# A joint first stage, a state-space scan whose inputs are fetched in the stage ahead of it, and a reordered preparation stage in a kernel of two networks

## What is computed

```python
# first block, layer 0: projections of x; attention with a bias by relative distance
proj = jnp.einsum('bsd,df->bsf', h, w_in)          # h is x, 1024 x 1024
bias = rel_bias[_t5_bucket(off * dilation)]
# second block: the conditioning vectors
sc, scc = jax.nn.silu(c), jax.nn.silu(c_ctx)[None]

def ssd_stream(z, xbc, dt_raw, ...):               # state-space branch
    xbc = silu(dwconv_centred(xbc, conv_w) + conv_b)
    xs, bm, cm = split(xbc)
    # forward and backward chunked scans of xs * dt, with the decays exp(cumsum(dt * a))
    y = y_f + flip(y_b) + d_skip[:, None] * xs
    return rms_norm(y * silu(z), norm_g)

def gdn_stream(qkv, gate, ...):                    # gated delta rule branch
    q, k = l2_norm(q) * 64 ** -0.5, l2_norm(k)
    ...                                            # both directions, one state per head
    return rms_norm(o_f + flip(o_b), norm_g) * silu(gate)
# the gdn branch walks the 16 x 64 grid of tokens by columns; its result is put back in raster order
lat = concatenate([pool_branch(...), s_lat, to_raster(g_lat)]) @ w_out
```

## Time and profile before

| | |
|---|---|
| median of 3 runs | 4337.53 us (4337.32 to 4341.66) |
| the profiled execution | 4332.35 us, of which 4330.8 us are the span from the first to the last instruction |
| mean granted TensorE clock over the span | 0.918 of full speed |
| PE busy, VectorE busy, ScalarE busy, GpSimd busy | 3677.2, 1645.7, 1081.7, 1009.2 us |
| start of the program to the first product of the projection | 0 to 46.0 us |
| `gdn_prepare` starts | 2930.4 us |
| `gdn_scan` loads start, `ssd_scan` starts, `pool_branch` starts | 3351.8, 3492.4, 3651.2 us |

### The profile page before, as it was taken

One profiled execution on the slowest core, in us unless ns is written; L12 is line 12 of the kernel. 1 busy time (PEld: TensorE's weight loads), 2 busy tenths in 40 slices (PEclk: granted clock), 3 DMA queues, 4 the chain that ended last, 5 costly groups with the idle time before them and its releaser, 6 DMA issues. The chain is left out here.

```text
span 4330.8 us, 47294 instructions
## 1 busy us (share of the span) xinstructions
PE 3677.2 (85%) x16689; PEld 2393.0 (55%) x16689; DVE 1645.7 (38%) x3931; ACT 1081.7 (25%) x2192; POOL 1009.2 (23%) x844
## 2 busy tenths in 40 slices
PE   7989998889798999999989598997867835757996
PEld 3635676667345566656568346574456834333442
DVE  1025552432442335345443251324478546141101
ACT  0023343332332233323321350221113111111111
POOL 0000000332341333333332353002222533111110
PEclk9989999899899999999999797998988857878998
DMA  3164532221531111111111532122325421445996
GB/s 97 63 182 140 167 101 80 95 69 55 213 128 49 43 57 42 58 38 39 43 59 44 232 130 78 44 70 89 117 79 179 158 82 35 173 172 200 319 324 218
DMA packets 413680, 494.03 MB, mean 114 GB/s; under 512 B 71298, under 2 KB 319386, under 8 KB 413459
## 3 DMA queue, kind: packets, MB, share of 16 engines
q1 hardware_dynamic: 384947, 457.61, 32.0%
q0 software_dynamic: 4608, 16.78, 1.5%
q10 hardware_dynamic: 23904, 16.78, 1.2%
HBM read 362.32 MB, written 128.77 MB: 113 GB/s over the span
## 5 line engine op out<-in xcount | busy, mean ns | idle before, releaser
L628 PE MATMUL hgrn_ps_w<-xT,hgrn_ring 128*128 128x512 f32 x1152 | 508.7, 597 | 0.0
L600 POOL TENSOR_TENSOR hgrn_queries<-hgrn_qd,hgrn_pair_decay 128x640 f32<-128x640 f32 x192 | 284.5, 1499 | 416.9 <-PE hgrn_ps_a L679 196.9
L628 PEld LDWEIGHTS hgrn_ps_w<-xT,hgrn_ring 128*128 128x128 f32 x1152 | 217.4, 193 | 252.4 <-issue 252.4
L624 PE MATMUL hgrn_ps_w<-hgrn_ring,xT 128*128 128x256 f32 x1536 | 337.9, 379 | 0.0
L624 PEld LDWEIGHTS hgrn_ps_w<-hgrn_ring,xT 128*128 128x128 f32 x1536 | 289.2, 190 | 38.2 <-issue 0.5
L780 DVE COPY_PREDICATED hgrn_scores<-hgrn_mask,hgrn_ps_s 128x128 f32<-128x128 uint32 x192 | 48.7, 297 | 469.9 <-issue 468.5
L352 PE MATMUL gla_bg_ps<-gla_bg_w,xT 128*128 128x256 f32 x768 | 195.8, 401 | 5.3 <-DMA gla_bg_w<-in_w_in_ab_dram 5.3
L352 PEld LDWEIGHTS gla_bg_ps<-gla_bg_w,xT 128*128 128x128 f32 x768 | 151.3, 202 | 38.7 <-issue 10.6
L1145 PE MATMUL end_ps_z<-end_w,end_yT 128*128 128x512 f32 x384 | 168.6, 599 | 1.6 <-ACT end_yT L1094 1.6
L878 ACT ACTIVATE hgrn_k_tok<-hgrn_ps_a 128x256 f32<-128x256 f32 x84 | 32.2, 383 | 547.9 <-PE hgrn_ps_a L654 547.9
L2292 PE MATMUL end_ps_z<-end_w,end_yT 128*128 128x512 f32 x384 | 167.4, 596 | 0.8 <-ACT end_yT L2220 0.8
(11 more groups left out here) (596 smaller groups left out, 6785.5 us busy)
## 6 DMA issues: line engine op xcount, KB each, us to landing
expw_wg<-in_exp_w_gate_dram SPq DMA_DIRECT2D x16, 2048.0 KB, 10.5
expw_wu<-in_exp_w_up_dram SPq DMA_DIRECT2D x16, 2048.0 KB, 16.2
expw_wd<-in_exp_w_down_dram SPq DMA_DIRECT2D x16, 2048.0 KB, 21.8
att_w_ada<-in_ada_w_dram SPq DMA_DIRECT2D x24, 1024.0 KB, 6.1
hgrn_ring<-in_w_in_c_dram SPq DMA_DIRECT2D x36, 512.0 KB, 4.0
end_gt<-gate_l SPq DMA_DIRECT2D x16, 768.0 KB, 7.4
hgrn_ring<-in_w_in_c_dram SPq DMA_DIRECT2D x12, 1024.0 KB, 5.4
hgrn_o<-hgrn_o_stage SPq DMA_DIRECT2D x192, 64.0 KB, 2.8
```

What stands on the lines that cost most here:

```text
L600: pool.tensor_tensor(queries[:, d, s, :].rearrange("p (b a c) -> p b a c", b=POINTS, a=PC), q, f, ALU.mult).then_inc(queries_done, 1)
L624: last = pe.matmul(bank[:, q * 2 * P:(q + 1) * 2 * P], xT[:, k, t * P:(t + 1) * P], wt[:, k, :], start=(k == 0), stop=(k == KB - 1))
L628: last = pe.matmul(bank[:, :], wt[:, k, 0:P], xT[:, k, part * BANK:(part + 1) * BANK], start=(k == 0), stop=(k == KB - 1))
```

## The change

Six edits, in the order of the program.

1. `transpose_in`, `bias_vectors` and `condition` become one stage, `prologue`. All eight tiles of x have a buffer of their own, so no load waits. The first two weight blocks of the projection, the conditioning vectors and the clearing of `vpad` are issued behind them on the same queue; the two tables come through ACT's queue. ACT copies every second bank. PE makes the three bias products after the fifth tile. `project` gets the two weight buffers already filled.
2. In `gdn_prepare` the first background weight block is asked for ahead of k and q, the other two behind; ACT's moves of the lead stand ahead of the roots.
3. `gdn_scan` stores each finished tile with one DMA of 128 partitions, in column order; `mix_and_route` reads `y_gdn` with two DMAs of 64 partitions per tile, in raster order.
4. Five of the six inputs of `ssd_scan` are loaded inside `gdn_scan`, one per step from the third on, behind that step's own loads. They lie in the memory of `hT`, which is free by then, and in one new tensor.
5. In `ssd_scan` the products `xdt` and `xw` are made unit by unit: four ahead, the others among the takes of the context units (DVE) and inside the loop over latent units (POOL), where the eight skip products stand too.
6. The gate's Silu stands behind the sixteen Exp on ACT and waits only for the gate.

```diff
+def prologue(nc, tag, src, dst, rel_bias, buckets, vectors, vpad, c, c_ctx, sT, weights, wbuf):
...
+        raw = sb("raw", [P, T, D])
...
+        @block.sync
+        def _(sp):
+            for t in range(T):
+                sp.dma_start(raw[:, t, :], src[t * P:(t + 1) * P, :]).then_inc(raw_loaded[t], 16)
+            for b in range(2):
+                sp.dma_start(wbuf[b][:, :, :], weights.rearrange("(k p) n -> p k n", p=P)[:, :, b * W:(b + 1) * W]).then_inc(w_loaded, 16)
...
+                sp.dma_start(cond[:, 0, :], c[0].rearrange("(k p) -> p k", p=P)).then_inc(cond_loaded, 16)
+                sp.dma_start(cond[:, 1, :], c_ctx.rearrange("(k p) -> p k", p=P)).then_inc(cond_loaded, 16)
+            sp.wait_ge(zeroed, 2)
+            for first in (0, P, VPAD + SEQ, VPAD + SEQ + P):
+                sp.dma_start(vpad[first:first + P, :], zero[:, :]).then_inc(stored, 16)
+            sp.wait_ge(w_loaded, 32)
...
+        @block.scalar
+        def _(act):
+            act.dma_start(rb[0:REL_BUCKETS, :], rel_bias).then_inc(bias_loaded, 16)
+            act.dma_start(bk[:, :], buckets).then_inc(bias_loaded, 16)
             for t in range(T):
...
+                act.activation(dst[:, 4:8, t * P:(t + 1) * P], ps[n % 5][:, :].rearrange("p (j c) -> p j c", j=4), ACT.Copy).then_inc(act_copied, 1)
+            act.wait_ge(cond_loaded, 32)
+            act.activation(sT[:, :, :], cond[:, :, :].rearrange("p r k -> p k r"), ACT.Silu)
+            act.wait_ge(scaled, 3)
+            act.dma_start(vectors, vec[:, :]).then_inc(stored, 16)
+            act.wait_ge(stored, 80)
...
+                if t == MIDDLE:
+                    pe.wait_ge(bias_loaded, 32)
+                    pe.wait_ge(zeroed, 2)
+                    for n in range(3):
+                        pe.matmul(ps_v[n][0:AH, 0:VEC], rb[:, :], bk[:, n * VEC:(n + 1) * VEC], start=True, stop=True).then_inc(made, 1)
...
             def load(job, i, u, f, before, column):
-
+                if u < held:
+                    return
...
@@ ssd_scan: POOL @@
-            pool.wait_ge(loaded, 96)
-            for d in range(2):
-                pool.wait_ge(xdt_done, T2 * (d + 1))
-                for t in range(T2):
-                    pool.tensor_tensor(by_head(xw[:, d, t, :]), by_head(xdt[:, d, t, :]),
-                                       spread(to_end[:, t, d * SH:(d + 1) * SH], SH, SE), ALU.mult).then_inc(xw_done, 1)
-            for t in range(TILES):
-                pool.tensor_tensor(by_head(Y[:, t, :]), by_head(xs[:, t, :]), spread(skip[:, :], SH, SE), ALU.mult).then_inc(y_set, 1)
...
+            for u in range(AHEAD):
+                weigh(u)
             for n in range(LAT_UNITS):
...
                 last.then_inc(sm_done, 1)
+                if n < LAT_UNITS - 2:
+                    weigh(n + AHEAD)
+                if n < TILES:
+                    skip_path(n)
                 if n:
                     pool.drain()
                     add(n - 1)
@@ ssd_scan: VectorE @@
+            weigh(0, AHEAD)
+            dve.wait_ge(consts, 1)
             args(0)
+            weigh(AHEAD, AHEAD + 4)
             for u in range(2 * CTX_STEPS):
                 take(u)
+                weigh(AHEAD + 4 + 3 * u, AHEAD + 7 + 3 * u)
@@ ssd_scan: ScalarE @@
-            act.wait_ge(loaded, 96)
-            act.activation(gate[:, :, :], gate[:, :, :], ACT.Silu).then_inc(gate_done, 1)
             for n in range(LAT_UNITS):
                 act.wait_ge(arg_done, n + 1)
                 act.activation(sm[:, n % 2, :, :], sm[:, n % 2, :, :], ACT.Exp).then_inc(exp_done, 1)
+            act.wait_ge(loaded, 16)
+            act.activation(gate[:, :, :], gate[:, :, :], ACT.Silu).then_inc(gate_done, 1)
@@ gdn_prepare @@
+            bg.load(sp, 0)
             for n, dst in ((1, k_n), (0, q_n)):
                 sp.dma_start(dst[:, :, :], tok[:, n * GW:(n + 1) * GW].rearrange("(t p) c -> p t c", p=P)).then_inc(loaded, 16)
-            bg.begin(sp)
+            for u in range(1, bg.ring):
+                bg.load(sp, u)
...
+            for g in range(LEAD):
+                bg.move(act, g)
             act.wait_ge(squared, 2 * T2)
             act.wait_ge(consts, 1)
             act.activation(std[:, :, :], norms[:, :, :], ACT.Sqrt, bias=eps[:, 0:1]).then_inc(std_done, 1)
-            for g in range(LEAD):
-                bg.move(act, g)
@@ gdn_scan @@
+                if 0 <= s - FIRST < len(next_loads):
+                    dst, src = next_loads[s - FIRST]
+                    sp.dma_start(dst, src).then_inc(fetched, 16)
...
-                    for w in range(P // GRID_H):
-                        sp.dma_start(y_out.rearrange("(r t w) c -> w r t c", t=TILES, w=P // GRID_H)[w, :, t, :],
-                                     O[w * GRID_H:(w + 1) * GRID_H, t, :]).then_inc(stored, 16)
-            sp.wait_ge(stored, 16 * TILES * (P // GRID_H))
+                    sp.dma_start(y_out[t * P:(t + 1) * P, :], O[:, t, :]).then_inc(stored, 16)
+            sp.wait_ge(stored, 16 * TILES)
+            sp.wait_ge(fetched, 16 * len(next_loads))
@@ mix_and_route @@
-                for src, dst in ((y_ssd, y[:, t % 2, 0, :]), (y_gdn, y[:, t % 2, 1, :]), (x, xt[:, t % 2, :])):
+                for src, dst in ((y_ssd, y[:, t % 2, 0, :]), (x, xt[:, t % 2, :])):
                     sp.dma_start(dst, src[rows, :]).then_inc(loaded[t % 2], 16)
+                for r in range(P // GRID_W):
+                    sp.dma_start(y[r * GRID_W:(r + 1) * GRID_W, t % 2, 1, :],
+                                 y_gdn.rearrange("(w r) c -> r w c", r=GRID_H)[t * (P // GRID_W) + r]).then_inc(loaded[t % 2], 16)
```

More of the change, by code:

```diff
@@ L173, in multiply @@
             def multiply(job, i, u, f, before, column):
-                wait(pe, w_loaded[u % 2], 16 * i + 16 * (u // 2 + 1))
+                wait(pe, w_loaded[u % 2], 16 * i + 16 * (u // 2 + 1) - 8 * held)
                 w = wbuf[u % 2]
@@ L2878, in by_head, with ssd_inputs, ssd_scan @@
     return t.rearrange("p (h e) -> p h e", e=width)
-def ssd_scan(nc, tag, tok, chan, z, d_skip, norm_g, dt, cum, from_start, to_end, whole, logs, y_out):
+def ssd_inputs(hT, bc_T, tok, chan, d_skip, norm_g):
     BC = 2 * N_STATE
+    flat = hT[:, :, :].rearrange("p k t -> p (k t)")
+    ends = (T2 * SW, T2 * (SW + BC), T2 * (SW + BC) + SH, T2 * (SW + BC) + SH + SW)
+    xs = flat[:, 0:ends[0]].rearrange("p (t c) -> p t c", c=SW)
+    b_tok = flat[:, ends[0]:ends[1]].rearrange("p (t c) -> p t c", c=BC)
+    skip, norm = flat[:, ends[1]:ends[2]], flat[:, ends[2]:ends[3]]
+    rows = lambda a: a.rearrange("(t p) c -> p t c", p=P)
+    loads = ((xs, rows(tok[:, 0:SW])), (b_tok, rows(tok[:, SW:SW + BC])), (bc_T[:, :, :], chan.rearrange("(k p) t -> p k t", p=P)),
+             (skip, row_to_all(d_skip, SH)), (norm, row_to_all(norm_g, SW)))
+    return (xs, b_tok, bc_T, skip, norm), loads
+def ssd_scan(nc, tag, inputs, z, dt, cum, from_start, to_end, whole, logs, y_out):
     HG = SH // 2 * SE
+    AHEAD = 2 * CTX_STEPS
     with ExitStack() as ctx:
@@ L2889, in ssd_scan @@
         pbank = lambda n: ctx.enter_context(nc.psum_tensor(f"{tag}_{n}", [P, BANK], F32))
[L2890 to L2891 removed]
+        xs, b_tok, bc_T, skip, norm = inputs
         gate = sb("gate", [P, TILES, SW])
[L2893 removed]
         mask = sb("mask", [P, 2, P])
@@ L3014, in _, with weigh @@
         def _(dve):
-            dve.wait_ge(loaded, 96)
-            dve.wait_ge(consts, 1)
-            for d in range(2):
-                for t in range(T2):
+            def weigh(first, last):
+                for u in range(first, last):
+                    t, d = place(u)
                     dve.tensor_tensor(by_head(xdt[:, d, t, :]), by_head(xs[:, t, :]), spread(dt[:, t, d * SH:(d + 1) * SH], SH, SE),
```

152 lines of the change are left out of this document (59 added, 93 removed).

## The result

| | before | after |
|---|---|---|
| median | 4337.42 us | 4256.06 us |
| fastest to slowest | 4328.48 to 4341.66 | 4250.86 to 4259.29 |
| profiled execution, its span | 4332.35, 4330.8 | 4256.28, 4254.6 |

What follows compares the result with a forecast made beforehand. Stages kept apart by barriers take turns waiting, with PE and DMA not full early on. Gains 21.0 + 7.6 + 9.9 - 0.3 + 31.3 = 69.5 us take 4332.35 to 4262.9, median 4268; range 4254 to 4284 (0.75), or to 4290.

Steps and rivals of the forecast that it cites:

- Start of the program: Joint first stage: bytes moved set its end, first product at 25.0 instead of 46.0 us; gain 21.0, bounds 17 and 22.5.
- Preparation: Delta rule's preparation: earlier weights and ACT moves bring the first turns 9.6 us earlier; gain 7.6 us, bounds 5 and 9.6.
- the price of PE's pause: Preparation: PE's pause of 8 us ahead of the loop costs about 2 us once more.
- Stores: Delta rule's end: 64 store issues become 8, next stage starts at 3482.5; gain 9.9 us, bounds 9 and 10.2.
- Fetching ahead: Delta rule's scan: loading 6.1 MB of state-space inputs there hides in free DMA time; cost 0, bounds 0 and 4 us.
- Held-up steps: Rival: added loads make one or two delta rule steps wait, total 4272 to 4276 us; chance 0.05.
- State-space scan: State-space stage: a shorter head less a longer loop; gain 31.3 us, bounds 23.5 and 38.
- The head: State-space scan's head: second unit's arguments at S+22.9 instead of S+60.2, 37.3 us less; bounds 34 and 41.
- The loop: State-space loop: `ssd_kept` waits for GpSimd's products, 6 us longer, between 3 and 10.5.
- Its signs: State-space loop: 5.2 to 5.8 us per unit for eight units, 5.1 to 5.4 behind, `ssd_kept` mean above 1 us.
- The rival in which VectorE waits for all of GpSimd's row: State-space loop: VectorE gets in only after GpSimd's whole piece, 41 us more instead of 6, total 4303; chance 0.10.
- the one in which all engines take turns: State-space loop: the three engines' work adds to 13.2 us per unit, 130 us more, total 4392; chance 0.02.

Runs made afterwards that it cites:

- e8: Changed kernel with the four padding stores moved into the projection and the bias table stored ahead of the conditioning vectors: first product at 22.53 us, median 4254.29 us.
- e7: Changed kernel with the preparation's 20 squares made by ACT and VectorE's drains there removed: stage 164.6 us, median 4244.02 us, ratio to before 0.9783.
- e12: Kernel before with ACT's moves ahead of the norms, weights still asked for behind k and q: preparation 175.6 us, ratio 0.9985.
- e11: Kernel before with only the delta rule's stores in raster order and the mixing stage's reads to match: stage 130.8 us, ratio 0.9978.
- e4: Kernel before with the state-space inputs fetched in the delta rule's scan, all products still made ahead of the loop: state-space stage 138.2 us, ratio 0.9949.
- e1: Kernel before with the joint first stage alone: first product at 25.35 us, ratio 0.9958.
- e3: Kernel before with xdt, xw and skip products made by unit, inputs still loaded at the state-space stage's start: stage 139.4 us, ratio 0.9952.
- e5: Changed kernel with one added GpSimd product per unit in 14 units of the state-space loop: loop 85.6 us, ratio to before 0.9833.
- e6: Changed kernel with three added GpSimd products per unit in 14 units of the state-space loop: loop 102.5 us, ratio to before 0.9876.
- e10: Changed kernel with six added GpSimd products per unit in the first eight state-space units, a row of eight: stage 154.3 us, ratio to before 0.9899.

## Why the prediction was right, and where its terms were off

The direction, the order of the terms and the range held; 76.1 us came for 69.5, and 4256 for 4268. Of these 12 us, 6.6 are gain beyond the forecast and 5.2 the allowance of the median over the profiled execution, which the kernel before had and the changed kernel has not. The stated range reaches down to 4254, so that it held with 2 us to spare, and in part by luck: the state-space scan gained more than its upper bound and the preparation less than its lower one. The lower sum of the bounds, 54 us, also leaves out the 4 us of the fetching; with them it is 50.

**Start of the program**, forecast 21.0, measured 20.7 and, alone, 20.6 (19.9 on average against all old starts). The sum of bytes was right: 340 to 426 GB/s, a hole of 1 us for the vectors. The padding, put at 3.0 us, adds 2.7 (e8); without it the vectors' slow way would set the end.

**Preparation**, forecast 7.6, measured 4.8 and 5.1, at or below the forecast's lower bound. The turns come 9.4 us earlier, as worked out (9.6), and VectorE's chain is what is late next. The step that failed is the price of PE's pause: 2 us were taken from the comparison of 16 records of a fill, and it is 4.4 (e7). The fill of the kernel before, from which the price came, stood behind a pause too, but PE was busy without a break behind it, the granted clock was at 0.95 again in the stretch from 2973 to 2974, and the decays that followed at 2978 took their 1.50 us. Here turns, a wait and decays follow, the clock stays at 0.50 beyond 2960, and turns, decays and the next fill take 0.90, 2.93 and 3.93 in place of 0.49, 1.50 and 2.74. And the forecast took both edits as gains. e12 shows that asking for the weights first costs 3.8 us: most of it because PE's wait moves from ahead of the fills to behind them, where the clock has come up and is lost again.

**Stores**, forecast 9.9, measured 10.2 in the changed kernel and in e11. The delta rule's stage shrank by 12.6; the other 2.5 us are scatter of the scan and no effect of the change.

**Fetching ahead**, forecast 0: the scans with it are no longer than those without. The cleanest pair is at the same granted clock of 0.87: 127.7 us in e4, which fetches, and 127.6 to 127.8 in e1, e3 and e11, which do not. Held-up steps, the rival, did not occur.

**State-space scan**, forecast 31.3, measured 40.0, above the bound of 38. Two steps were mis-sized. The head: 20.0 us in place of 22.9, since I held VectorE's three `xdt` back until GpSimd's row was over; they took turns and ended at 3468.26, at S+12.1 in place of S+14.8. The loop: 0.5 us in place of 6. Its signs failed with it: a unit took 5.09 us in the first eight and 5.03 behind, below the 5.2 to 5.8 and 5.1 to 5.4 that were named, and `ssd_kept` 0.80 us on average, not above 1. Its median was 0.85 us before and 0.84 after. The Trainium skill, "SBUF — State Buffer", section "SBUF: two separate sides", says that a VectorE operation with two SBUF inputs and a GpSimd one exclude each other for a whole instruction. In the loop the traces of the changed kernel, e5, e6 and e10 agree with a wait for one instruction (at most 1.42 us for a product of 0.56, never two instructions of 0.8); ahead of it the 4.45 and 5.22 us passed several. I had weighed the 4.44 us of the earlier trace rows against the rule and added to it. But even the 3 us that I got from the rule alone were too many, as the loop has slack: where `ssd_kept` took 1.02 and 0.84 us, two units took 5.51 + 4.55 us, and where it took 0.56 twice, 5.05 + 5.04. Only the one of 1.42 cost 0.4. (The bound of 10.5 us for the loop is 10.4 by its own terms.) The rival in which VectorE waits for all of GpSimd's row is out for the loop by e10, the one in which all engines take turns by the loop's 81.57 us.

**Untouched stages** took 2 us more than in the execution before, within the scatter of 2881.7 to 2888.1 us. By the profiled executions the account closes: 8.7 us more than forecast from the state-space scan, 2.7 from the delta rule's and 0.5 from mixing, less 2.8 in the preparation, 0.3 at the start and 2.2 in between, are 6.6, which is what the forecast of 4262.9 for this execution was off by.

## What to carry to other kernels

In this kernel a wait of TensorE cost more than its length where the clock had come up ahead of it: put the unavoidable wait ahead of a stretch of work, not into it, and ask of every earlier start what it will then wait for. Products that one engine makes for another went into a loop at next to no cost as long as the engine's whole work per turn, 4.6 us, stayed below the turn of 5.05, and fetching in a stage where the DMA engines were free for 0.63 of the time cost nothing that could be seen. Measure a small gain in its own stage: a scatter of several us in another one hid e12's and e8's.
